# Attention of a transformer trunk: dense products dealt to the softmax steps anew, the next queries copied two steps later

## What is computed

```python
N_HEADS = 16; HEAD_DIM = 64; CHUNK = 64; LEFT_CHUNKS = 8; BAND = 576
qkv = (h @ w_qkv).reshape(bsz, seq, 3, N_HEADS, HEAD_DIM)
def one_chunk(c):      # 64 queries see their own chunk and 8 before it
    s = einsum('bqhd,bkhd->bhqk', qc, kc) * scale + bias
    p = softmax(where(valid, s, -inf))
    return einsum('bhqk,bkhd->bqhd', p, vc)
return o @ w_out       # added to x
```

## Time and profile before

| | |
|---|---|
| runs | 2762.26 us median of 3 (2761.03 to 2767.27) |
| profiled execution | 2762.53 us, span 2760.7 us |
| TensorE busy | 95% of the span |
| VectorE, ScalarE, GpSimd busy | 46%, 24%, 29% |
| attention | pairs start at about 1391.7 us; the last ends at about 1998 us |
| mean granted TensorE clock | 0.985 of full speed |

### The profile page before, as it was taken

One profiled execution on the slowest core, in us unless ns is written; L12 is line 12 of the kernel. 1 busy time (PEld: TensorE's weight loads), 2 busy tenths in 40 slices (PEclk: granted clock), 3 DMA queues, 4 the chain that ended last, 5 costly groups with the idle time before them and its releaser, 6 DMA issues.

```text
span 2760.7 us, 33357 instructions
## 1 busy us (share of the span) xinstructions
PE 2621.3 (95%) x12148; PEld 2157.7 (78%) x12148; DVE 1266.8 (46%) x2092; ACT 654.3 (24%) x1219; POOL 799.4 (29%) x450
## 2 busy tenths in 40 slices
PE   6999999999999999999879999999789999999997
PEld 5878888877888888888667777777668888888885
DVE  7225555566222222222856556556773333222225
ACT  3112111122000000000455555555630000000002
POOL 3223322233333333333212221122133333333335
PEclk9999999999999999999989999999999999999998
DMA  4223211111111111111100110111011111111101
GB/s 138 97 88 111 72 59 59 65 41 51 46 53 53 46 46 46 46 46 46 40 33 31 40 36 23 38 40 40 24 46 54 46 46 46 46 53 53 46 31 61
DMA packets 53221, 143.50 MB, mean 52 GB/s; under 512 B 5392, under 2 KB 15776, under 8 KB 53168
## 3 DMA queue, kind: packets, MB, share of 16 engines
q1 hardware_dynamic: 35632, 119.71, 12.7%
q10 hardware_dynamic: 17536, 23.07, 2.5%
HBM read 130.13 MB, written 12.63 MB: 52 GB/s over the span
## 4 chain that ended last, share of the span: by engine, by line
PE 87%; DVE 9%; ACT 2%; issue 2%; DMA 0%; DVEq 0%; SPq 0%; ACTq 0%
PE bank L442 18%; PE bank L444 18%; PE bank L443 18%; PE scores L442 4%; PE scores L443 4%; PE scores L444 4%; PE probs_t L444 4%; PE probs_t L443 4%; PE probs_t L442 4%; PE probs_t L607 2%; DVE full L968 2%; DVE prob L1203 1%; PE scores L598 1%; PE bank L630 1%; PE bank L629 1%
## 5 line engine op out<-in xcount | busy, mean ns | idle before, releaser
L442 PE MATMUL bank<-hn_hi,w_hi 128*128 128x512 f32 x2048 | 811.9, 396 | 28.2 <-DVE hn_lo L973 23.8
L444 PE MATMUL bank<-hn_hi,w_lo 128*128 128x512 f32 x2048 | 802.1, 392 | 0.0
L443 PE MATMUL bank<-hn_lo,w_hi 128*128 128x512 f32 x2048 | 801.1, 391 | 0.0
L360 POOL TENSOR_SCALAR w_hi<-raw 128x1024 fp32r<-128x1024 f32 x212 | 247.3, 1167 | 1897.4 <-PE bank L444 1322.4
L362 POOL TENSOR_TENSOR w_lo<-raw,w_hi 128x1024 fp32r<-128x1024 f32 x212 | 519.7, 2451 | 17.7
L442 PEld LDWEIGHTS bank<-hn_hi,w_hi 128*128 128x128 f32 x2048 | 386.9, 189 | 112.7 <-DVE hn_lo L973 18.2
L444 PEld LDWEIGHTS bank<-hn_hi,w_lo 128*128 128x128 f32 x2048 | 386.5, 189 | 82.2
L443 PEld LDWEIGHTS bank<-hn_lo,w_hi 128*128 128x128 f32 x2048 | 387.0, 189 | 77.8 <-issue 1.2
L1043 DVE TENSOR_TENSOR full<-bank,atmp 128x512 f32<-128x512 f32 x88 | 60.9, 692 | 715.7 <-ACT atmp L821 714.1
L821 ACT ACTIVATE atmp<-bank 128x512 f32<-128x512 f32 x88 | 52.6, 598 | 1152.4 <-PE bank L444 1152.4
L1052 DVE TENSOR_TENSOR x<-probs_t,x 128x512 f32<-128x512 f32 x240 | 162.7, 687 | 110.5 <-PE probs_t L444 110.3
(11 more groups left out here) (138 smaller groups left out, 3593.3 us busy)
## 6 DMA issues: line engine op xcount, KB each, us to landing
raw<-w_units_in SPq DMA_DIRECT2D x212, 512.0 KB, 3.2
v_raw<-v_scratch ACTq DMA_DIRECT2D x16, 512.0 KB, 4.0
bias<-rel_scratch ACTq DMA_DIRECT2D x8, 640.0 KB, 3.7
x<-x_t_in SPq DMA_DIRECT2D x16, 256.0 KB, 6.5
v_scratch<-atmp ACTq DMA_DIRECT2D x16, 256.0 KB, 2.5
v_scratch<-full ACTq DMA_DIRECT2D x16, 256.0 KB, 2.7
out_t<-x SPq DMA_DIRECT2D x16, 256.0 KB, 2.0
ws_raw<-w_s_t_in ACTq DMA_DIRECT2D x8, 64.0 KB, 1.8
```

Source lines behind the costliest of these rows:

```text
L360: pool.tensor_scalar(w_hi[slot][:, :], raw[r][:, :], 1.0, 1.0, ALU.mult, ALU.mult).then_inc(w_split, 1)
L442: pe.matmul(out, lh, rh, start=start, stop=False)
L443: pe.matmul(out, lh, rl, start=False, stop=False)
L444: last = pe.matmul(out, ll, rh, start=False, stop=stop)
```

## The change

The dense products of the middle pairs are dealt to other steps; the last pair keeps the old table of `OUT0` under another name. ScalarE's and VectorE's copies of the first half of the next queries stand in step 16, not in 14. Below, the second part is TensorE's, the third ScalarE's, the fourth and fifth VectorE's.

```diff
         V_1 = {0: (0, 1, 2), 1: (3, 4, 5, 6), 2: (7,)}
-        OUT1P = {3: (0, 1), 4: (2,), 5: (3, 4), 6: (5,), 7: (6, 7)}
-        OUT0 = {13: (0, 1), 14: (2,), 15: (3,), 16: (4,), 17: (5,), 18: (6,), 19: (7,)}
-        NEXT_Q = [{8: (0,), 9: (1, 2), 11: (3, 4), 13: (5, 6), 14: (7,)}, {16: (0,), 17: (1, 2), 18: (3, 4), 19: (5,)}]
+        OUT1P = {3: (0,), 4: (1, 2), 5: (3,), 6: (4, 5), 7: (6,), 8: (7,)}
+        OUT0 = {13: (0,), 14: (1,), 16: (2, 3), 17: (4,), 18: (5,), 19: (6, 7)}
+        OUT0_LAST = {13: (0, 1), 14: (2,), 15: (3,), 16: (4,), 17: (5,), 18: (6,), 19: (7,)}
+        NEXT_Q = [{8: (0,), 10: (1, 2), 12: (3, 4), 13: (5,), 14: (6,), 15: (7,)}, {17: (0, 1), 18: (2, 3), 19: (4, 5)}]
...
-                    for n in OUT0.get(m, ()):
+                    for n in (OUT0_LAST if last else OUT0).get(m, ()):
                         if n == 0:
                             pe.wait_ge(w_split, (u + (3 if last else 4)) * 2 + 2)
                             pe.wait_ge(o_lo_done, it * 2 + 1)
...
-                    if m == 14 and not last:
+                    if m == 16 and not last:
                         query_hi(it, 0)
...
-                    if m == 14 and not last:
+                    if m == 16 and not last:
                         query_lo(it, 0)
...
-                    for n in OUT0.get(m, ()):
+                    for n in (OUT0_LAST if last else OUT0).get(m, ()):
                         out_add("out0", 0, n)
```

## The result

The changed kernel takes 2773.24 us (median of 4, 2772.25 to 2776.62) for 2762.15 before: ratio 1.0039, 95% interval 1.0021 to 1.0056, slower by 11 us. Forecast were 2776 us, with 2758 to 2790 as the range. The profiled execution has a span of 2772.4 us for 2760.7.

What follows compares the result with a forecast made beforehand. TensorE is busy 95% of the span, so only its gaps can be won. From 2762.3 us, +9.7 for the pairs and +4.5 for the clock gave 2776 us, range 2758 to 2790.

Steps and rivals of the forecast that it cites:

- T(13): Transposes of step 13, standing in step 16: forecast at 1897.66 for 1901.91, 2.85 us gained by then.
- The copy: Step 16, then 17: second half's first query product waits for its bank until T(13)+5.73, a new 2.75 us wait.
- ready but in order: Step 17: values, output product 4 and next transposes behind the query product's wait were called ready, held only by TensorE's order.
- The end of the pair: Step 19: next keys wait for bank 0, output product 6's, starting +4.4 after the values end; 1.6 us wait.
- The lower bound: Pair's end: the keys' wait was given as 1.4 to 2.1 us, keys starting between +4.15 and +4.9.
- The sum for a pair: Middle pair: 2.75 + 1.6 - 2.85, a loss of 1.45 us (1.2 to 1.95); six pairs +8.7.
- The last pair: Keeps the old out0, has no queries; its 1.44 us wait behind step 8 takes up a product: -0.7 us.
- The clock: Granted clock falling behind the new wait: four falls of 1.6 for two of 1.06, +4.5 us; bounds -2.1 to +20.
- Faster: Rival, 0.11: query bank and bank 0 are free when asked for, so the gains remain; time 2742 us.
- equal: Rival, 0.15: one of the two new waits is missing, 2.85 against 2.75 per pair; time 2759 to 2766 us.
- Slower still: Rival, 0.14: the 2.75 us idle lowers the clock each time; time 2781 to 2792 us.
- The products' move does nothing: Rival, 0.02: even steps' waits turn up in odd ones, leaving the copy's 1.8; 6 us more, 2782.

Runs made afterwards that it cites:

- early_only: Kernel before with only the new tables for steps 3 to 12 (previous pair's output products, next queries); copy stays in step 14: 2747.3 us, ratio 0.9945.
- copy_before_gather: Changed kernel with ScalarE's half of the queries' copy ahead of its gathering moves in step 16: 2768.7 us.
- q_from_18: Changed kernel with the second half's first two query products out of step 17, three in 18 and three in 19: 2791.1 us.
- both_mended: Changed kernel with the copy in step 15, query products 6 and 7 in 14, output product 1 in 15 and 6 in 18: 2747.1 us, ratio 0.9947.
- add6_first: Changed kernel with VectorE's add of output product 6 ahead of o_full and o_lo in step 19: 2762.5 us.
- late_only: Changed kernel with the early tables (steps 3 to 12) of the kernel before: 2789.4 us, ratio 1.0103.
- fill15: early_only with middle pairs' output products a step earlier from step 15 on (3 and 4 in 15, none in 19): 2741.8 us, ratio 0.9928.
- copy15_out1_in13: both_mended with output product 1 in step 13 instead of 15: 2746.0 us.
- gather_first: Changed kernel with VectorE's add of the previous pair's output product 7 behind o_full in step 8: 2780.3 us, run again 2780.8.

## Why the prediction was right

**T(13) and the early steps.** Forecast 4.25 us earlier in the pair; it is 4.38 (42.53 us behind the pair's first scores for 46.91). Step 9's scores came 0.98 earlier (0.8 forecast), step 13's 1.80 (1.7). early_only shows the early half as a gain of 2.0 us a pair (76.6 to 74.6), where 1.65 were expected.

**The copy.** The query product starts at T(13)+5.71 for +5.73, a wait of 2.73 by starts for 2.75. copy_before_gather, which shortened the chain, confirms the cause. Wrong was the remark on what stands behind the wait ("ready but in order"). It changed no number, but would have misled whoever tried to fill the wait: in q_from_18 the values behind it wait 0.9 us longer than the query product did.

**The end of the pair.** The values end at 1766.78, T(13)+14.65, as laid out; the keys at +4.24 for +4.4; wait 1.42 for 1.6. `o_lo` took 0.69 and not 1.44: GpSimd's split began at 1769.98, 0.54 us behind its start, as forecast. In both_mended, where product 6 is back in step 18, `o_lo` at the end takes 1.45 again. The lower bound was the right one.

**The sum for a pair** was +1.45 and is +1.25 (77.85 less 76.6): six pairs 7.5 for 8.7. Pair 0 is 1.0 longer, but before it holds one of the two falls (1.07, taken as in pair 4), and after it holds none: without that it gives +2.1 for +1.7. The last pair gives -1.75 for -0.7. The term for it left out how its own low stretches fell: the mean granted clock over it is 0.90 before and 0.93 after.

**The clock**, the weakest term: four falls of 1.6 for two of 1.06. That is +4.3; the prediction wrote +4.5. The profile has three falls of 1.3 (79.15 less 77.85) for two of 1.07: +1.8. Count and size were both too high. The size of 1.55 does appear in add6_first (77.85 less 76.3) and late_only (81.36 less 79.8). It isn't a shorter wait behind that makes the difference, since the bank wait of late_only is 1.26 us as here. Here the low stretch begins while TensorE still waits; in pair 5 it goes on at 1835.71:

```profile
1835.20:1835.70 0.50, 0.00 (x0) 0.00 (x0) 0.47 (x2) 0.00 (x0) 0.00 (x0) 0.50 0.00 0
```

In pair 4 of late_only TensorE goes on at 1766.3 and the clock falls 1 us later, so the whole low stretch costs work:

```profile
1766.40:1767.30 0.90, 0.90 (x4) 0.76 (x5) 0.84 (x3) 0.00 (x0) 0.00 (x0) 1.00 0.00 0
1767.40:1770.00 2.60, 2.60 (x12) 2.42 (x11) 1.89 (x4) 0.83 (x1) 0.00 (x0) 0.50 0.00 0
```

**How near the total is.** The terms measured are 7.5 + 2.1 + 1.8 for pairs 0 to 6 (11.4; by the profile 11.3) and -1.75 for the last pair. To these come 1.45 us ahead of the stage and 0.7 behind it, which no term had. So the time within 3 us of the forecast is in part luck: terms too high by some 5 us stand against 2 us from elsewhere and a pair 0 that was too low. The two waits and their sizes are not luck.

**The rivals.** "Faster" and "equal" fell when both waits came. "Equal" named a real point: with only the boundary wait taken away the kernel is equal to before (add6_first). "Slower still" (a fall each time) holds for the 3.38 us waits of q_from_18, seven of seven, not for the 2.48 us waits: three of seven here, and five at most in the other kernels that have them. "The products' move does nothing" fell with early_only.

## What to carry to other kernels

Filling idle steps with independent work has two bills besides the steps: who empties the accumulator that the work writes, and where that stands in the emptying engine's own order. Before a read is moved later, list the next writer of its bank and everything queued behind the read; here three waits of the kind cost 1.3 to 2.7 us a pair each, and two of them hid a gain of 2 us a pair that the early tables had. Once the waits are known, put ready work into the one that can't be removed, as fill15 does, and split a change into halves before you drop it.

## What the runs showed of the hardware

The granted clock's falls came at the same pairs in two profiles each of two kernels. A reorder of two VectorE instructions, which costs a pair 0.15 us, moved pairs 0 to 6 by 6.7 us, 5.7 of them through the falls; the whole kernel moved by 4 us on one chip.

How often a fall came behind the wait in the late steps, in pairs 0 to 6:

| wait, us | kernel | falls of seven |
|---|---|---|
| 0.84 | fill15 | 0 |
| 1.09 | copy15_out1_in13 | 0 |
| 1.32 | both_mended | 0 |
| 1.53 | copy_before_gather | 4 |
| 1.64 | before, early_only | 2, 2 |
| 2.48 | after, add6_first, late_only, gather_first | 3, 4, 5, 5 |
| 3.38 | q_from_18 | 7 |

The wait's length alone doesn't give the count: 1.53 us has more falls than 1.64, and 2.48 has three to five. A fall costs a pair 1.05 us (early_only, 75.69 less 74.64) to 1.6 (copy_before_gather, 78.48 less 76.9), and the longer ones of gather_first cost 2.8 (80.8 less 78.0). In the changed kernel, where the low stretch begins inside the wait, it is 1.3.

VectorE's `o_lo`, 512 columns from two SBUF inputs, takes 0.69 us, or 1.45 with GpSimd's split already running beside it; in the changed kernel, whose `o_lo` starts half a us ahead of the split, it is 0.69 even though the two overlap at its end.
